# One core, a hybrid retention and attention block: projections by seven block products in a phase of their own, retention and attention after them with operands from DRAM

## The reference

```python
B, S, D = 1, 1024, 1024;  RET_HEADS, RET_DK, RET_DV = 4, 128, 256;  FOX_HEADS, FOX_DH = 8, 128;  D_FF = 2816
mod = silu(c) @ ada_w + ada_b                      # six vectors sh1 sc1 g1 sh2 sc2 g2
h = modulate(rms_norm(x, norm1_w), sh1, sc1)
z = h @ w_in                                       # 1024 x 8200
rq, rk, rv, rg, fq, fk, fv, ff, gr, gf = split(z)  # 512 512 1024 1024 1024 1024 1024 8 1024 1024
rq = rotary(rq, pos);  rk = rotary(rk, pos) * (RET_DK ** -0.5)
ro = retention(rq, rk, rv)        # chunks of 64, decay gamma_h^|t-s|, state carried from chunk to chunk
ro = ro * rsqrt(mean(ro * ro, per head) + EPS)
y_ret = silu(rg) * ro
log_f = log_sigmoid(ff + b_f)
y_fox = forgetting_attention(fq, fk, fv, log_f)    # causal softmax of q.k/sqrt(d) + F_t - F_s, F = cumsum(log_f)
merged = sigmoid(gr) * (y_ret @ ret_proj) + sigmoid(gf) * (y_fox @ fox_proj)
x = x + g1 * (merged @ w_out)
h2 = modulate(rms_norm(x, norm2_w), sh2, sc2)
x = x + g2 * ((silu(h2 @ w_gate) * (h2 @ w_up)) @ w_down)
return rms_norm(x, norm_f_w)
```

## Time and profile before

| What | Value |
|---|---|
| median of 3 runs | 2063.22 us |
| the profiled execution, its own time | 2063.27 us |
| its span (first to last instruction) | 2061.5 us |
| TensorE busy | 1895.3 us, 92% |
| VectorE, GpSimd, ScalarE busy | 53%, 51%, 31% |
| granted TensorE clock, mean | 0.969 of full |
| DMA | 224.91 MB, mean 109 GB/s |
| instructions | 23857 |

### The profile page before, as it was taken

The page is one execution under the profiler, slowest core; times in us unless marked ns, Lnnn a source line. Parts: engine busy times, 40 slices in busy tenths (PEclk is TensorE's granted clock), DMA queues, the critical chain, the costliest instruction groups (busy, mean ns, idle before and its releaser), DMA issues.

```text
span 2061.5 us, 23857 instructions
## 1 busy us (share of the span) xinstructions
PE 1895.3 (92%) x8788; PEld 1564.2 (76%) x8788; DVE 1097.0 (53%) x1576; ACT 637.1 (31%) x1159; POOL 1061.0 (51%) x584
## 2 busy tenths in 40 slices
PE   2889999999799999999999999669999999769996
PEld 2676888888688888888888888448888888557785
DVE  4875545555555555546545434373564555435536
ACT  4430232323232222333211110544444444221212
POOL 2522526262723343334345574367887887378662
PEclk9998999999999999999999999789999999879998
DMA  9370202011411111111132220403444544488553
GB/s 355 102 240 23 62 22 60 23 52 31 140 35 51 41 31 51 41 41 41 41 143 62 72 72 23 151 2 106 161 149 146 162 153 143 162 329 307 211 183 143
DMA packets 157395, 224.91 MB, mean 109 GB/s; under 512 B 5500, under 2 KB 118012, under 8 KB 153988
## 3 DMA queue, kind: packets, MB, share of 16 engines
q1 hardware_dynamic: 151766, 200.99, 29.8%
q10 hardware_dynamic: 5554, 22.92, 3.0%
HBM read 170.90 MB, written 52.99 MB: 109 GB/s over the span
## 4 chain that ended last, share of the span: by engine, by line
PE 78%; DVE 8%; DMA 4%; POOL 3%; ACT 3%; issue 2%; SPq 1%; DVEq 0%; ACTq 0%; POOLq 0%
PE ps L739 50%; PE ps L1173 8%; PE ps L1175 8%; PE ps L1174 8%; PE ps L1067 1%; DMA b_ada_ring<-in_ada_w 1%; DVE b_res L1707 1%; DMA f_units<-b_fu 1%; POOL b_db L708 1%; DVE b_act_q L1707 1%; DMA b_macc<-in_ada_w 1%; POOL b_db L702 1%; DVE b_probs L1707 1%; POOL b_wu L650 1%; ACT b_db L1664 1%
## 5 line engine op out<-in xcount | busy, mean ns | idle before, releaser
L739 PE MATMUL ps<-b_hT,b_w_split 128*128 128x512 f32 x3120 | 772.5, 398 | 15.3 <-DVE b_fk L1945 9.5
L739 PEld LDWEIGHTS ps<-b_hT,b_w_split 128*128 128x128 f32 x3120 | 574.5, 190 | 130.1 <-issue 11.2
L586 POOL TENSOR_TENSOR b_spare<-b_w_stage 1x1 f32<-1x1 f32 x89 | 28.2, 317 | 728.2 <-PE ps L739 655.1
L1173 PE MATMUL ps<-b_act_q,b_wu 128*128 128x512 f32 x616 | 244.4, 397 | 19.5 <-POOL b_wu L650 9.6
L587 POOL TENSOR_SCALAR b_w_split<-b_w_stage 128x1024 fp32r<-128x1024 f32 x89 | 246.8, 2773 | 0.2 <-issue 0.2
L1174 PE MATMUL ps<-b_act_q,b_wu 128*128 128x512 f32 x616 | 241.7, 392 | 0.0
L1175 PE MATMUL ps<-b_act_q,b_wu 128*128 128x512 f32 x616 | 241.7, 392 | 0.0
L589 POOL TENSOR_TENSOR b_w_split<-b_w_stage,b_w_split 128x1024 fp32r<-128x1024 f32 x89 | 220.7, 2480 | 7.4
L650 POOL TENSOR_TENSOR b_wu<-b_raw,b_wu 128x512 fp32r<-128x512 f32 x110 | 162.5, 1486 | 61.6 <-ACT b_wu L1552 61.1
L1173 PE MATMUL ps<-b_db,b_da 128*128 128x512 f32 x308 | 123.7, 402 | 40.9 <-issue 22.2
L1173 PEld LDWEIGHTS ps<-b_act_q,b_wu 128*128 128x128 f32 x616 | 116.7, 189 | 49.5 <-DVE b_act_q L1707 11.0
(11 more groups left out here) (208 smaller groups left out, 3014.0 us busy)
## 6 DMA issues: line engine op xcount, KB each, us to landing
f_units<-b_fu SPq DMA_DIRECT2D x77, 512.0 KB, 2.7
b_w_stage<-in_w_in SPq DMA_DIRECT2D x65, 512.0 KB, 4.1
b_da<-f_units SPq DMA_DIRECT2D x14, 2048.0 KB, 10.2
b_macc<-in_ada_w SPq DMA_DIRECT2D x13, 1024.0 KB, 4.8
b_raw<-in_w_gate SPq DMA_DIRECT2D x22, 512.0 KB, 4.8
b_raw<-in_w_up SPq DMA_DIRECT2D x22, 512.0 KB, 6.1
b_da<-f_units SPq DMA_DIRECT2D x7, 1536.0 KB, 6.4
b_ada_ring<-in_ada_w SPq DMA_DIRECT2D x10, 1024.0 KB, 9.6
```

The costliest lines, as they stand in the source:

```text
L586: pool.tensor_tensor(spare[0:1, :], src[0:1, 0:1], src[0:1, 0:1], ALU.add)
L739: return pe.matmul(o, l, r, start=start, stop=stop)
L1173: pe.matmul(o, l[0], r[0], start=begin and at == 0, stop=False, skip_group_check=go_on)
```

## The change

The program is rebuilt in phases.

- **A table `JOBS`** lists pairs of tiles. The 64 input tiles form 32 pairs, each with the seven products of the feed-forward stage: four pairs of silu gates, four of rotated q and k, eight of v, eight of branch gates and eight of attention's q and k. `ret_proj` and `fox_proj` follow with four pairs each, and the output matrix has block products too, by chunks as the down product. Each pair is a slot on TensorE (`pair_slot`). The ring of weight units has 8 places for 10.
- **Evacuation.** The results of pair p-1 are finished in slot p: combined in `cb`, activated, rotated or turned, split into hi and lo in `ost`, a ring of four, and stored in DRAM (`d_rqk`, `d_kd`, `d_rv`, `d_fqk`, `d_fv`, `d_silu`, `d_gate`). The turns of v and of the decayed keys go through one PSUM bank, 6; each waits for the one before it to be split (`turned`).
- **Later modulation and forget gates** run inside this phase.
- **Retention** then runs alone, four heads, and **attention** alone, eight heads, with operands read from DRAM a head ahead. The rows of head h+1 stand between the steps of head h (`row_at`). The division of the probabilities moves from VectorE to GpSimd. Both store units of their result in DRAM (`y_units`).
- **Then** `ret_proj`, `fox_proj`, the gates and the sum, the output matrix, norm 2 with a first product block by block (`first_pair`, now also used at the start), the gate and up products, and the down product in chunks of 3, 4 and 4 pairs.

```diff
-RING = 10
-CHUNKS = [(0, 4), (4, 4), (8, 3)]
...
+    JOBS.append(("v", O_FV + 2 * _i * P, O_FV + (2 * _i + 1) * P, 4 + _i))
+    JOBS.append(("gate", O_GF + 2 * _i * P, O_GF + (2 * _i + 1) * P, 4 + _i))
+for _h in range(FH):
+    JOBS.append(("qk", O_FQ + _h * P, O_FK + _h * P, _h))
+P_RET = len(JOBS)
+P_FOX = P_RET + 4
+P_GU = P_FOX + 4
+P_END = P_GU + FT
+for _i in range(4):
+    JOBS.append(("retp", 2 * _i, 2 * _i + 1, _i))
+for _i in range(4):
+    JOBS.append(("foxp", 2 * _i, 2 * _i + 1, _i))
+for _i in range(FT):
+    JOBS.append(("ffn", _i, _i, _i))
...
+OUTS = {"silu": [(s, 0) for s in range(4)], "gate": [(s, 0) for s in range(4)],
+        "v": [(s, 0) for s in range(4)], "qk": [(s, 0) for s in range(4)],
+        "rope": [(0, 0), (1, 0), (1, 1), (2, 0), (3, 0), (3, 1)]}
+OUT0, LOW0, ROT0, TRV0 = [0], [0], [0], [0]
+for _p in range(P_RET):
+    _k = JOBS[_p][0]
...
+OST = 4
...
+CHUNKS = [(0, 2), (2, 2), (0, 3), (3, 4), (7, 4)]
...
         @block.tensor
         def _(pe):
...
-            def job_part(bank, place, half, m0, m1):
-                for m in range(m0, m1):
-                    k, which = m // 3, m % 3
-                    w = w_split[:, place[0], int(which == 2), blk(k)]
-                    a = hT[:, int(which == 1), k, half * HALF:(half + 1) * HALF]
-                    last = mm(ps[:, bank, :], w, a, m == 0, m == 23)
-                return last
...
+            def first_pair(ph):
+                p = STARTS[ph]
...
+                    last.then_inc(h_tr, 1)
+                for j in range(4):
+                    transposes(0, j)
+                for k in range(HK):
+                    for u in range(Q7):
+                        if k + 1 < HK and u in (0, 1, 3, 4):
+                            transposes(k + 1, (0, 1, 3, 4).index(u))
+                        if k == 0:
+                            pe.wait_ge(u_rdy, Q7 * p + u + 1)
+                            if u == 0 and ph == 0:
+                                pe.wait_ge(s_modT, 1)
+                        pe.wait_ge(h_lo, 28 * ph + Q7 * k + u + 1)
...
+            def pair_slot(p, between=None):
+                X, Y, Z = banks(p)
+                for u in range(Q7):
+                    bank = (X, Y, X, Z, X, Y, X)[u]
+                    pe.wait_ge(u_rdy, Q7 * p + u + 1)
+                    if p == P_RET or p == P_FOX:
+                        pe.wait_ge(q_ld[u], 16 if p == P_RET else 32)
+                    if u in (0, 1, 3):
+                        bank_free(p, u)
+                    elif u == 2:
+                        pe.wait_ge(c_snap, 3 * p + 1)
+                    elif u == 4:
+                        pe.wait_ge(c_snap, 3 * p + 3)
+                    elif u == 5:
+                        pe.wait_ge(c_snap, 3 * p + 2)
+                    else:
+                        pe.wait_ge(c_comb, 3 * p + 2)
+                    for k in range(HK):
+                        last = pair_part(p, bank, u, k, u in (0, 1, 3))
+                    last.then_inc(u_used, 1)
+                    if between:
+                        between(u)
+            turned = []
+            def evac(p, u):
+                if p < 0:
+                    return
+                kind = kind_of(p)
+                if kind == "v" and u < 4:
+                    s, low = u, LOW0[p] + u + 1
+                    if s < 3:
+                        pe.wait_ge(c_comb, 3 * p + s + 1)
+                    else:
+                        pe.wait_ge(c_fin, p + 1)
+                elif kind == "rope" and u in (2, 4):
+                    s = u - 1
+                    low = LOW0[p] + 3 * (u // 2)
+                    pe.wait_ge(e_rot, ROT0[p] + s + 1)
+                else:
+                    return
+                if turned:
+                    pe.wait_ge(e_lo, turned[-1])
+                else:
+                    pe.wait_ge(c_fin, 1)
+                for b in range(4):
+                    last = pe.transpose(ps[:, 6, blk(b)], cb[:, p % 2, s, blk(b)], ident)
+                last.then_inc(e_tr, 1)
...
-                    next_part(fill[n], fill[n + 1])
...
+                        p_transposes(h, n + 1)
+                    if n in row_at and h + 1 < FH:
+                        rows(h + 1, row_at[n])
+                    p_times_v(h, n)
+            for p in range(P_RET, P_GU):
+                pair_slot(p)
...
         @block.gpsimd
         def _(pool):
...
+            def normed(h, t):
+                at0 = t * (t + 1) // 2 * P
+                pool.wait_ge(a_r, 8 * h + t + 1)
+                p = probs[h % 2][:, at0:at0 + (t + 1) * P]
+                pool.tensor_scalar(p, p, smax[:, h % 2, 3, t:t + 1], None, ALU.mult).then_inc(a_p, 1)
...
         @block.scalar
         def _(act):
...
+            def pair_slot(p, end):
+                for u in range(Q7):
+                    if p + 1 < end:
+                        weight_hi(Q7 * (p + 1) + u)
+                    if u < (2 if p in STARTS else 3):
+                        snapshot(p, u)
+                    evac(p - 1 if p not in STARTS and p != P_RET else -1, u)
+                if p not in STARTS:
+                    act.wait_ge(u_used, Q7 * p + 7)
+                    cb_free(act, p)
+                    copy(cb[:, p % 2, 3, :], ps[:, banks(p)[0], :]).then_inc(c_fin, 1)
...
+            def prob_hi(h, n):
+                g, s = ((0, n) if n < 4 else (1, n - 4))
+                N = 12 * h + n
+                act.wait_ge(a_pt, N + 1)
+                if N >= 3:
+                    act.wait_ge(a_pv, N - 2)
+                c0 = max(0, s - 4 * g) * P
+                copy(pT2[:, n % 3, 0, c0:], ps[:, 4 + n % 2, c0:]).then_inc(a_pthi, 1)
...
```

3485 lines of the change are left out of this document (1729 added, 1756 removed).

## The result

The changed kernel takes 2485.48 us (median of 4 runs, 2482.28 to 2486.02), beside 2063.11 us of the kernel before: 1.2045 times as long, 95% interval 1.2024 to 1.2066. The forecast of 2168 us had the sign and missed the size: the loss is 422 us and not 105. The profiled execution has a span of 2483.5 us.

A forecast was written before the change was run, and what follows sets the result against it. TensorE bounds the kernel, busy 1895.3 of 2061.5 us. Ten stage terms sum to a 2166 us span, so 2168 us, 5.1% slower: 116 us of work saved, 221 of new waiting; range 2095 to 2245.

The forecast's parts named there:

- The step that failed: Retention and attention: DRAM reads of 512 KB transfers issued a head ahead cost nothing; without that cover some 5 us an entry.
- The second step that failed: TensorE's granted clock: retention heads at 25 us as granted, 23.5 at full clock; attention with no clock loss counted.
- attention's 131 us: Attention alone: forecast 276 us, at 32.4 us a head over seven passes and 23 for the first rows; bounds 175 and 340.
- The 54 us of the projections: Projection phase: forecast 686 us, from 31 slots of 18.85, 46 for v turns, 34 for rotation, 22 for modulation and forget gates.
- Retention's 42: Retention alone: forecast 101 us, ScalarE's queue setting a head at 25 us, the first 17, entry 9; bounds 80 and 140.
- The output tiles' 61: Eight output tiles after attention: forecast 160 us, as 151 and about 9 for the second operand.
- The row of output matrix and norm: Output matrix, norm 2 and first feed-forward product: forecast 86 and 94 us, 180 together.
- The start: Start to the end of the first blockwise product: forecast 120 us, with ScalarE free of weight units and norm at 52.
- The 0.68 us at 225.18: Projection phase: a VectorE operation with two SBUF sources takes 0.68 us alone and 1.63 beside GpSimd.
- The first: Rival, chance 0.13: queue waits overlap and TensorE stays the pace; attention heads at 19.8 us for 32.4, total 2072 or 2000.
- The third: Rival, chance 0.10: GpSimd sets the pace of the projections at 20.5 us a slot; 2230 us in all.
- The second, the clock: Rival, chance 0.17: retention and attention granted clock 0.50, adding 45 and 16 us; 2229 us in all.

The follow-up runs named there:

- e5: On top of e1, ScalarE takes the high part of the next turned block ahead of the row's exponential in attention; 2344.60 us, 73.6 below e1.
- e1: Changed kernel with attention's reads of q, k and forget bias let go a head earlier, only v waiting as before; 2418.18 us, 67.3 off.
- e4: Changed kernel with ScalarE taking a turned v block's high part ahead of the snapshot of the running product; 2433.09 us, 52.4 off.
- e12: Changed kernel with the rotation of retention's q and k done on 8 columns in place of 512; 2438.86 us, 46.6 off.
- e3: Changed kernel with the constants of the four retention heads in buffers of their own, read before the phase; 2471.31 us, 14.2 off.
- e8: Changed kernel with the stores of attention's last seven units ahead of 6 MB of activation reads in the transfer queue; 2480.84 us, 4.6 off.
- e7: Changed kernel with VectorE combining the running slot's products ahead of the previous pair's units, behind attention-projection and feed-forward pairs; 2472.09 us, 13.4 off.
- e2: Changed kernel with 72 additional TensorE matmuls of 128 x 128 at the start of each attention head after the first; 2495.75 us, 10 us slower.
- e6: On top of e3, retention heads 2 and 3 read nothing and compute with the operands of heads 0 and 1; 2469.86 us, 1.5 below e3.

## Why the prediction was wrong

**What held.** The sign, and that a head of attention goes by waits in the order of the queues and not by TensorE or GpSimd. The 516 matmuls are saved (6528 for 7044), and a slot with nothing beside it is 19.0 us, as the feed-forward slots of before. The forget gates and the later modulation take 22 us, as forecast (8 in the first slot, 14 in the last). The chain in an attention head is that of the prediction: a row, its exponential, the high and the low part one behind the other. e5, which takes the exponential out of it, shows it. The 1.99 us of the v slots were forecast as 2.0. Of the signs named, TensorE under 65% busy in attention came (217 of 407 us) and no other engine above it; the length of the phase, of the v slots and of the start did not.

**The step that failed.** "The reads from DRAM are 512 KB transfers issued a head ahead; I cost them at nothing". I had the rate of the queues and not the moment at which they are let go. Two buffers are enough where the consumer works on one head; here the rows work a head ahead of the weighted sums, both buffers are in use, and the read starts when it should have ended. Measured: 70.6 us of waits, 67.3 us by e1. The line that releases the buffers was before me: the wait on `a_pv` for all seven reads, where only v needs it.

**The second step that failed.** The sum has the lower clock as 1.5 us in each of three retention heads and nowhere else; as a rival it had 61 us. An estimate of its size from the page: 116 us of matmuls are gone, so at the pace of before TensorE would be busy for 1895.3 - 116 = 1779 us, and it is for 1925.5, 146 us more for the same work. Not all of that is time lost, since TensorE waits in any case where others set the pace. In the v and the rotation slots, where e4 and e12 take the waits away, the clock goes back to 1.00, and its share is 1.6 to 5.2 us a slot, as worked out there.

**Terms that were too small.** The other 61 of attention's 131 us: 28 in seven passes (37.5 us a head with the units, the waits taken off, for 33.5), 32 in the first rows, which wait for retention's last units and stores and for the second head's reads (55 us for 23). The 54 us of the projections: 28 in the v slots (28.1 us each for 24.6), of which the waits were right and most of the rest is the clock behind them; 20 in the four rotation slots (32.0 us for 27), which is what the estimate for one of them gives for the clock (5.2). Retention's 42: 14 of them are waits for constants that stand last in the list of reads (e3); the rest is open as said. The output tiles' 61: 24 at the entry for 9, 15 in the first slot of `fox_proj`, where TensorE waits four times for 1.7 to 3.1 us, mostly for GpSimd's weight units (I take its 14 MB of reads to be behind them, which was not tried), and 29 in the three slots behind it, in which the waits for VectorE's combination are 9.0, 6.9 and 6.1 us; e8 took back some 5, and most of what e7 gained there the output matrix lost again. The row of output matrix and norm hides two misses of opposite sign: the output matrix takes 116.5 us for 86, with one wait of 19.1 us for VectorE's part of a weight unit (`b_wb`), and norm and first product take 75.0 for 94. That the two nearly cancel is luck; of the 94, its terms 72.8 and 12 give only 85. The feed-forward's 28: I took its order for that of before; VectorE's queue has the units ahead of the combination now, and e7 gave 17 back. The down product's 10 were not looked into.

**Terms that were too large.** The start, 100.1 us for 120. I take it that the first block product overlaps the weight units better than I had it; no run tests that.

**A row that was misread.** The 0.68 us at 225.18 is not VectorE alone: GpSimd has an operation with one input running all through it, and beside the same kind VectorE also took 1.49 us (at 210.32). The value holds all the same, since it is 0.68 at 74.83 too, where GpSimd is idle. So a busy GpSimd alone does not slow such an operation; at 208.59, where VectorE takes 1.63, GpSimd has one with two inputs.

**The rivals.** The first (waits don't add, TensorE stays the pace) is refuted by the heads, which take 46.2 to 51.9 us where it wanted under 24; with the changes of e1 and e5 the heads without units do come to 23.6 to 24.1. The third (GpSimd the pace) is refuted too: the projection slots without turn or rotation behind the first take 19.0 to 20.0 us, but for the last one, which has the forget gates. The second, the clock, came about in part: 0.67 in retention and 0.73 in attention, where I had given it 0.17 and a price of 61 us. The Trainium skill's TensorE: Matmul & The Clock Gate (A second HAM failure mode: psum-queue depth-cycling) says that micro-idles of TensorE between groups of matmuls, if they are frequent enough, make the clock go back and forth between its two levels. The rows of attention agree (0.73), and e5, with fewer and shorter waits, has 1.00 in a head without units. It is a consequence of waits here, and multiplies what each of them costs. I had treated the clock as a case apart, and not as a factor on each wait.

**The range.** Its upper end of 2245 took in one rival at a time. Of the stages only the start came out shorter. I take it that the others share a cause, work that was hidden before and is not now, and that their risks should have been added up; the experiments show the waits one by one and not that common cause.

## What to carry to other kernels

Where a kernel is cut into phases, ask of each buffer when it is let go and when it is wanted next, not how long its transfer takes; with a consumer that works ahead, give each operand the wait of its own last reader. In a phase without filler on TensorE, the order within the queues of the other engines is worth more than the arithmetic: one swapped line was 74 us, another 52. And a wait of TensorE can cost more than its length, when what follows runs at the lower clock: 1.99 us twice were 5.9 to 7.6 us a slot (e4).

## What the hardware showed unexpectedly

- In four of seven waits, 72 matmuls of 128 x 128 without a gap took 15.0 to 15.6 us at a granted clock of 0.50 to 0.53; in the other three they ran at 1.00 (e2). In e5 a head with TensorE busy for 19.9 us of 24.0 had 1.00.
- Behind the second of two waits of 1.99 us, 3.4 us apart, the granted clock was 0.57 over 4 us, though TensorE was busy; behind the first it was 1.00.
- Leaving out 12 MB of reads took the DMA share from 0.76 to 0.40 over three retention heads and changed the time by 1.5 us (e6).
